# The context's half of a residual add on GpSimd, x's half as a scalar_tensor_tensor on VectorE

## What is computed

```python
def rmsnorm(x, g):
    xf = x.astype(jnp.float32)
    y = xf * lax.rsqrt(jnp.mean(xf * xf, axis=-1, keepdims=True) + NORM_EPS)
    return (y * g.astype(jnp.float32)).astype(x.dtype)

def modulated_norm(h, g, m, k):
    return rmsnorm(h, g) * (1.0 + m[..., k + 1, :]) + m[..., k, :]

def gated_residual(h, y, g, m, k, weight):
    return h + weight * m[..., k + 2, :] * rmsnorm(y, g)
```

## Time and profile before

| | |
|---|---|
| median of 3 runs | 2761.61 us (2759.4 to 2763.28) |
| profiled execution | 2760.84 us |
| its span, first to last instruction | 2759.1 us |
| mean granted TensorE clock | 0.952 of full speed |
| PE busy / PE weight load | 2533.0 / 2129.8 us |
| VectorE (DVE) busy | 1610.4 us |
| ScalarE (ACT) busy | 1040.4 us |
| GpSimd (POOL) busy | 0.2 us, four memsets at the start |
| bytes read from HBM | 346.41 MB, 126 GB/s over the span |

### The profile page before, as it was taken

One profiled execution on the slowest core, in us unless ns is written; L12 is line 12 of the kernel. 1 busy time (PEld: TensorE's weight loads), 2 busy tenths in 40 slices (PEclk: granted clock), 3 DMA queues, 4 the chain that ended last, 5 costly groups with the idle time before them and its releaser, 6 DMA issues.

```text
span 2759.1 us, 35165 instructions
## 1 busy us (share of the span) xinstructions
PE 2533.0 (92%) x14190; PEld 2129.8 (77%) x14190; DVE 1610.4 (58%) x2859; ACT 1040.4 (38%) x1731; POOL 0.2 (0%) x4
## 2 busy tenths in 40 slices
PE   5999998987999999899999888998998968998978
PEld 4888875874678888588887667998998758998658
DVE  7767745268477673576233555555466467466466
ACT  3222324237432222422222545444444434444433
POOL 0000000000000000000000000000000000000000
PEclk9999999999999999999999998999999879999879
DMA  6554531210135543145222112553544204544202
GB/s 255 196 200 183 190 146 48 90 62 1 65 123 198 197 183 122 46 183 198 92 94 105 61 46 83 193 189 123 191 153 153 77 2 151 192 152 153 77 1 92
DMA packets 48689, 349.72 MB, mean 127 GB/s; under 512 B 5392, under 2 KB 5520, under 8 KB 6544
## 3 DMA queue, kind: packets, MB, share of 16 engines
q1 hardware_dynamic: 48528, 347.48, 34.2%
HBM read 346.41 MB, written 1.05 MB: 126 GB/s over the span
## 4 chain that ended last, share of the span: by engine, by line
PE 84%; DVE 11%; ACT 3%; issue 2%; DMA 1%; SPq 0%; DVEq 0%; ACTq 0%
PE ps L402 24%; PE ps L403 23%; PE ps L404 23%; PE ps L468 2%; DVE yT L1365 1%; PE ps L544 1%; PE ps L546 1%; PE ps L545 1%; PE ps L587 1%; DVE w_lo L1318 1%; PE ps L574 1%; DVE small L1463 1%; DVE hT L1376 1%; DVE conv L1659 1%; ACT w_hi L914 1%
## 5 line engine op out<-in xcount | busy, mean ns | idle before, releaser
L914 ACT ACTIVATE w_hi<-ring 128x1024 fp32r<-128x1024 f32 x504 | 533.7, 1060 | 1258.9 <-PE ps L404 1193.3
L1318 DVE TENSOR_TENSOR w_lo<-ring,w_hi 128x1024 fp32r<-128x1024 f32 x504 | 616.4, 1224 | 647.2 <-ACT w_hi L914 645.3
L402 PE MATMUL ps<-u_hi,w_hi 128*128 128x512 f32 (+1 forms) x1744 | 635.8, 365 | 33.8 <-DVE u_lo L1333 20.3
L403 PE MATMUL ps<-u_lo,w_hi 128*128 128x512 f32 (+1 forms) x1744 | 635.0, 364 | 0.0
L404 PE MATMUL ps<-u_hi,w_lo 128*128 128x512 f32 (+1 forms) x1744 | 631.8, 362 | 0.0
L402 PEld LDWEIGHTS ps<-u_hi,w_hi 128*128 128x128 f32 x1744 | 330.7, 190 | 95.3 <-issue 26.4
L404 PEld LDWEIGHTS ps<-u_hi,w_lo 128*128 128x128 f32 x1744 | 331.0, 190 | 52.5
L403 PEld LDWEIGHTS ps<-u_lo,w_hi 128*128 128x128 f32 x1744 | 331.1, 190 | 51.0 <-issue 0.2
L402 PE MATMUL ps<-uh,w_hi 128*128 128x256 f32 x1184 | 337.2, 285 | 29.9 <-ACT zt L1195 17.0
L1306 DVE CUSTOM_DVE_ANT_0 waste<-ring,condb,cols 128x1024 f32<-128x1024 f32 x280 | 346.3, 1278 | 0.2 <-DMA ring<-in_wk 0.2
L404 PE MATMUL ps<-uh,w_lo 128*128 128x256 f32 x1184 | 333.8, 282 | 0.0
(11 more groups left out here) (267 smaller groups left out, 2755.1 us busy)
## 6 DMA issues: line engine op xcount, KB each, us to landing
ring<-in_wk SPq DMA_DIRECT2D x324, 1024.0 KB, 4.9
hT<-in_x SPq DMA_DIRECT2D x1, 2048.0 KB, 17.7
htabs<-in_htabs SPq DMA_DIRECT2D x1, 1152.0 KB, 7.3
condb<-in_crow SPq DMA_DIRECT2D x1, 1024.0 KB, 5.2
out_t<-uT SPq DMA_DIRECT2D x1, 1024.0 KB, 3.9
trig<-in_trig SPq DMA_DIRECT2D x3, 256.0 KB, 6.5
wuk<-in_uk SPq DMA_DIRECT2D x2, 256.0 KB, 5.2
wuv<-in_uv SPq DMA_DIRECT2D x2, 256.0 KB, 6.7
```

Of the source, the lines that this page charges most:

```text
L402: mm(bank, hi, x_hi, start=first, stop=False)
L403: mm(bank, hi, x_lo, start=False, stop=False)
L914: f(half_hi(K, 0, HALF), ringed(n, K % 2 * HALF, (K % 2 + 1) * HALF), ACT.Copy).then_inc(whi_ready, 1)
L1318: tt(half_lo(K, 0, HALF), ringed(HALF_SLOT[K], K % 2 * HALF, (K % 2 + 1) * HALF), half_hi(K, 0, HALF).bitcast(F32), ALU.subtract).then_inc ...
```

## The change

In `post`, the residual step of the first block, VectorE keeps the multiplies of both halves. `x`'s half of `h` is added by a `scalar_tensor_tensor` with the constant 1.0 in place of a `tensor_tensor`. The context's half is added by GpSimd, which gets a program of its own: five times eight adds of 128x256, each behind a wait for the multiply of its piece. They count a new semaphore, `hctx_ready`; ScalarE's `squares` waits for it too where T = TT, and VectorE's `pre` waits for all eight before it begins. `h_ready` now counts only the adds of `x`'s half. For the residual after `sub` 5, which has only `x`, the form of the add is all that changes.

```diff
@@ sync
-                    sp.wait_ge(h_ready, 5 * 2 * KC + KC)
+                    sp.wait_ge(h_ready, 6 * KC)
@@ scalar
-            def squares(T, ready, seen, step_of, to=sq, src_stride=TT):
+            def squares(T, ready, seen, to=sq, src_stride=TT):
                 for c in range(KC):
                     if ready is not None:
-                        act.wait_ge(ready, seen + (c + 1) * step_of)
+                        act.wait_ge(ready, seen + c + 1)
+                    if ready is h_ready and T == TT:
+                        act.wait_ge(hctx_ready, seen + c + 1)
                     f(to[:, c * src_stride:c * src_stride + T], hT[:, c * src_stride:c * src_stride + T],
                       ACT.Square).then_inc(sq_ready, 1)
@@ vector, pre
                 dve.wait_ge(mod_ready, sub + 1)
                 dve.wait_ge(rstd_ready, norms)
+                if sub:
+                    dve.wait_ge(hctx_ready, KC * sub)
@@ vector, post
                         dve.wait_ge(t_ready, t_n + j - behind + 1)
                         if sub == 5:
 
-                            dve.wait_ge(h_ready, 5 * 2 * KC + (c // 2 + 1 if c else 0))
-                        tt(hT[:, to:to + S], hT[:, n:n + S], yT[:, n:n + S], ALU.add).then_inc(h_ready, 1)
+                            dve.wait_ge(h_ready, 5 * KC + (c // 2 + 1 if c else 0))
+                        if s == 0:
+                            stt(hT[:, to:to + S], yT[:, n:n + S], 1.0, hT[:, n:n + S], ALU.mult,
+                                ALU.add).then_inc(h_ready, 1)
@@ gpsimd, new
+        @block.gpsimd
+        def _(pool):
+
+            seen = 0
+            for sub in range(5):
+                seen += 2 * KC
+                for c in range(KC):
+                    n = c * TT + S
+                    pool.wait_ge(t_ready, seen + 2 * c + 2)
+                    nc.gpsimd.tensor_tensor(hT[:, n:n + S], hT[:, n:n + S], yT[:, n:n + S],
+                                            ALU.add).then_inc(hctx_ready, 1)
+                seen += 2 * KC
```

More of the change, by code:

```diff
@@ L273, in program @@
         h_ready = sem("h_ready")
+        hctx_ready = sem("hctx_ready")
         rot_done = sem("rot_done")
@@ L1052, in _ @@
                 T = S if sub == 5 else TT
-                squares(T, h_ready if sub else None, h_seen - KC * (TT // S), TT // S)
+                squares(T, h_ready if sub else None, h_seen - KC)
                 if sub == 0:
@@ L1135, in _ @@
                 t_seen += KC * (T // S)
-                h_seen += KC * (T // S)
+                h_seen += KC
             for lay in range(DEPTH):
                 if lay:
-                    squares(S, v_free, v - KC, 1, sq2, S)
+                    squares(S, v_free, v - KC, sq2, S)
                 else:
-                    squares(S, h_ready, h_seen - KC, 1, sq2, S)
+                    squares(S, h_ready, h_seen - KC, sq2, S)
                 norm(S)
```

## The result

The changed kernel takes 2760.0 us (median of 20 runs, 2755.8 to 2772.2) against 2751.52 us for the kernel before (20 runs, 2744.93 to 2763.28): 1.0032 of it, with a 95% interval of 1.002 to 1.0044. It is slower, by about 9 us. The time lies in the range, but the forecast said 13 us faster: it went to the other side. The forecast had added its change to the 2761.61 us of three runs, 10 us above the median of the 20.

The account below looks back on a forecast made before the run. VectorE's residual at five boundaries was taken as the bound. Gains of 10.2 us in four and 2.9 in the fifth, 13.1 off 2760.84, gave 2747.7; with 0.8 for the median, 2749 us, range 2744 to 2777.

Parts of the forecast that it names:

- What bounds the kernel: At five boundaries VectorE's residual ends last, so a microsecond less there is one less of the kernel, if stages stay unchanged.
- The three-operand form: VectorE's x adds: no extra time with a constant; other bound 0.07 us an add, 3 us in all.
- GpSimd's add: Context's add: 0.69 us, between 0.42 and 1.22, plus 0.1 us for both semaphore hops.
- The step that failed: In each boundary chunk GpSimd's add, 0.69 us plus 0.1, fits under VectorE's 1.13 us, so GpSimd keeps up.
- w: Time for which each GpSimd add holds VectorE up; seven such holds stand before a boundary's last multiply.
- rival (1): Each GpSimd add holds VectorE up, as both read SBUF: gain 13.1 - 35 w, 2773 us with 0.69; chance 0.30.
- rival (3): Half-way hold of VectorE, w between 0.22 and 0.53: gain melts to within 5.5 us either way, 2761; chance 0.12.
- The point from which it decides: Hold of VectorE per GpSimd add from which rival (1) decides: w = 0.37 us.
- a poor sign: Against rival (1): a second SBUF stream costs VectorE no set-up, 418 ns against 419 with one operand in PSUM.
- Rival (2): VectorE, without gaps, keeps GpSimd out until its x adds, in three boundaries its low() too, end: +22 us, 2784; chance 0.06.
- TensorE's 0.99 us a chunk: Sums of squares in a boundary: with squares 1.13 us apart TensorE doesn't queue, gaining another 0.35 us.
- The waits: Added waits of ScalarE and of VectorE before pre cost nothing; low() stays covered, SP's wait names the same add.

Follow-up runs that it names:

- no_context_add: Changed kernel without GpSimd's program and its waits, the context's half of h not added in the first five steps: 0.9982 of the kernel before, repeated 0.9971.
- gpsimd_one_input: Changed kernel with GpSimd's add replaced by a 128x256 copy from the constant table, context's add left out: one execution, 2750.03 us.
- gpsimd_behind: Changed kernel with GpSimd's eight adds of each step waiting for VectorE's last x add: one execution, 2797.61 us.
- the wide add, the dead half and the fill together: Kernel before with 512-column adds on VectorE, context's unread half dropped after sub 4, constant matmuls in TensorE's pauses: 0.9945 of the kernel before.

## Why the prediction was wrong

**What bounds the kernel**: right for time added. The boundaries are VectorE's residual, and what it gained in length the kernel did too (+6.4 by the profile, +9 timed with 5.5 to 12). For time taken away it is less sure: boundaries 12.2 and 9.5 us shorter gave 5 and 8 us (no_context_add and its repeat).

**The three-operand form**: right. With a constant and two SBUF tensors it takes 410 to 422 ns, 416 at the median, where no GpSimd add runs (no_context_add), against 418 for two operands. The half throughput that the Trainium skill's Vector Engine (DVE) Microarchitecture Reference (section Points that are easy to get wrong) gives it is not there.

**GpSimd's add**: 0.69 us by itself, as forecast; since that was the row of another engine with twice the columns, the digit is luck. Its two hops were put at 0.1 together and cost 0.18: the multiply ends at 448.98, the add starts at 449.06 and ends at 449.90, the square starts at 450.00. That is worth 0.1 us a boundary at most.

**The step that failed** is "It is under the 1.13 us that VectorE needs for a chunk, so GpSimd keeps up". It laid GpSimd's add beside VectorE's adds and multiplies at no cost to them, that is w = 0, and had a chance of 0.52. The chunk took 1.66 us. What took the step's place is rival (1), at w = 0.53 in place of the whole 0.69, because of GpSimd's 0.90 the first 0.24 lie before the `x` add's start and the last 0.13 no longer hold it (0.90 - 0.24 - 0.53). Its formula gives 13.1 - 35 x 0.53 = -5.5; the boundaries say -6.4. The pieces fit in the first one: the last multiply starts at 448.51 - 436.55 = 11.96 where 8.31 was forecast, 3.65 later, and the seven holds, one of 0.48 on a multiply and six of 0.53 on `x` adds, are 3.66. The price was at the edge of rival (3), and the mechanism, exclusion, was rival (1), which had 0.30 with a time of 2773. That the time lies in the range says little: the range took in both rivals. What compares is the change, forecast as -13, at most 5.5 either way by rival (3), +11 by rival (1), and measured as +9. A second point bears the formula out: a hold of 0.19 (gpsimd_one_input) gives 13.1 - 35 x 0.19 = 6.4, and the boundaries there are 5.8 shorter than before. The point from which it decides, 0.37, lies between the two and was not run itself.

**The weight** given against rival (1) rested on a poor sign: that a second SBUF input costs VectorE no set-up in a kernel where GpSimd is idle says nothing of what happens when GpSimd wants it too. The rule of the Trainium skill's SBUF — State Buffer (section Who interferes with whom) holds in every run here for which instructions exclude each other: two SBUF inputs on VectorE and a reading GpSimd instruction do (0.94 and 943 ns against 0.42), one SBUF input does not (0.41), a GpSimd instruction that only writes does not (0.42). Not quite the whole instruction held: the last 0.13 us of GpSimd's did not.

**Rival (2)**, VectorE never lets go, was wrong for the changed kernel: GpSimd had its turn in each chunk, though in the first one only after the `x` add. In gpsimd_behind VectorE did keep its turn over both `low()`.

**TensorE's 0.99 us a chunk** was mis-sized: 0.86 at the upper level of the clock and 1.71 at the lower, where some of a boundary's first chunks lie. Alone it would have cut the gain, 3.0 us a boundary with GpSimd free, to between 1.3 and 2.7 (no_context_add and its repeat), and, by the boundaries of the two sets, the 15 us to 12.2 and 9.5; with a chunk of 1.66 the sums had caught up before the last one, and it did not matter.

**The waits**: `pre` and SP's queue showed no new idle time, as said. The last context add did delay the `low()` by 0.52, covered by the wait for `rstd`.

## What to carry to other kernels

Work moved to GpSimd from a busy VectorE is free only where the two don't read together: before moving an elementwise add, look whether VectorE's instructions beside it have two SBUF inputs, and subtract nearly the whole overlap (0.53 of 0.66 us here). Ask first whether the work is needed at all (leaving out a dead half made the fifth boundary 6 us shorter, where the second engine made the kernel slower), and see what TensorE's clock does to the step that becomes the bound once the first one is shortened: a sum that takes 0.86 us a chunk at the upper level and fits under squares 1.13 apart takes 1.71 at the lower and does not.

## What the runs showed of the hardware

- A VectorE instruction with two SBUF inputs and a GpSimd one that reads SBUF exclude each other, and mostly the one that starts first goes first: a multiply in flight held GpSimd's add for 0.2 (0.90 against 0.69), that add then held VectorE's for 0.53; VectorE's two passes ahead by 0.17 us held GpSimd's for 2.06. The exception is the first chunk of each boundary of the changed kernel, where the `x` add went ahead of a GpSimd add that had started 0.24 us before it (1.23 us).
- GpSimd, 128x256 float32: add 0.68 us from start to start alone, mostly 0.84 to 0.92 beside VectorE and 1.23 in the exception above; copy 0.53 to 0.60 beside it, memset 0.31.
- In no_context_add TensorE stood idle for some 4 us before the squares of a boundary (3.94 and 3.84 in the rows), its granted clock fell from 1.00 to 0.50 in the pause or up to 1.4 us behind its end and stayed there for 3.4 or 6.8 us; a 512-column pass started every 0.85 us then and every 0.43 after. Matmuls of constants in the pauses kept the clock at 1.00. Without the context's add that took the time from 0.9982 and 0.9971 to 0.9916 of the kernel before; the wide add, the dead half and the fill together took 15 us of 2757.
- Two executions of one program differed by 10 us in span with boundaries equal to 0.1 us.
